# Attention scores: one operation per head for bias, maximum and sink in place of wide operations over four heads

## The reference, cut to what matters

```python
def windowed_gqa(q, k, v, sink, bias):
    ...
    s = jnp.einsum('bnqhgd,bnjhd->bnhgqj', qb, kb) * (HEAD_DIM ** -0.5) + bias
    s = jnp.where(jnp.asarray(valid)[None, :, None, None], s, -1e30)
    sink6 = sink.astype(jnp.float32)[None, None, :, :, None, None]
    m = jnp.maximum(jnp.max(s, axis=-1, keepdims=True), sink6)
    pe = jnp.exp(s - m)
    den = jnp.sum(pe, axis=-1, keepdims=True) + jnp.exp(sink6 - m)
    o = jnp.einsum('bnhgqj,bnjhd->bnqhgd', pe / den, vb)
```

## Time and profile before

| what | us |
|---|---|
| median of three runs | 1793.28 (1780.39 to 1795.96) |
| the profiled execution, its own time | 1783.18 |
| its span in the trace | 1781.1 |
| PE busy over the span | 1677.9 |
| DVE busy over the span | 904.8 |
| ACT busy over the span | 590.2 |
| first score matmul of the attention to the last `att_tok` | 651.8 to 787.8 |

### The profile page before, as it was taken

How to read it: one execution, slowest core, us unless ns; L and a number is a source line. 1 busy time by engine, 2 the same in 40 slices (tenths; PEclk the granted TensorE clock), 3 DMA queues, 4 the chain that set the end, 5 groups by cost and what they waited for, 6 DMA issues and landing times. The chain is left out here.

```text
span 1781.1 us, 26275 instructions
## 1 busy us (share of the span) xinstructions
PE 1677.9 (94%) x10034; PEld 1384.5 (78%) x10035; DVE 904.8 (51%) x998; ACT 590.2 (33%) x1015; POOL 409.2 (23%) x285
## 2 busy tenths in 40 slices
PE   7999999999999989999899999997999999997997
PEld 6878888877877767778788887885777777785786
DVE  5202777202044127742799325223777879952674
ACT  5211222231111126652344334113534343442332
POOL 1011111111111101002210022000265655653330
PEclk9999999999999989999789999998999999999999
DMA  6211222233455322107866434224767778744452
GB/s 222 78 58 60 80 79 80 100 90 117 133 183 169 118 74 62 32 31 234 261 198 166 165 126 138 83 72 146 297 224 256 276 280 303 282 170 142 142 189 95
DMA packets 117275, 267.70 MB, mean 150 GB/s; under 512 B 13044, under 2 KB 60868, under 8 KB 117181
## 3 DMA queue, kind: packets, MB, share of 16 engines
q1 hardware_dynamic: 101212, 211.60, 36.5%
q0 software_dynamic: 8320, 30.43, 5.1%
q10 hardware_dynamic: 7648, 24.35, 3.8%
HBM read 194.27 MB, written 72.07 MB: 150 GB/s over the span
## 5 line engine op out<-in xcount | busy, mean ns | idle before, releaser
L2228 DVE TENSOR_TENSOR ex_wlo<-ex_raw,ex_whi 128x1024 fp32r<-128x1024 f32 x102 | 156.1, 1532 | 7.6 <-ACT ex_whi L2222 4.3
L2224 DVE CAST ex_whi<-ex_raw 128x1024 fp32r<-128x1024 f32 x96 | 110.3, 1149 | 43.4 <-DMA ex_raw<-experts 38.5
L2816 PE MATMUL rt_p<-ex_whi,ex_xh 128*128 x280 | 113.6, 406 | 14.0 <-DVE ex_wlo L2228 8.6
L271 PE MATMUL rest_p<-hi_h,whi_in 128*128 128x512 f32 (+1 forms) x480 | 121.1, 361 | 0.0
L271 PE MATMUL rest_p<-lo_h,whi_in 128*128 128x512 f32 (+1 forms) x480 | 119.7, 357 | 0.0
L271 PE MATMUL rest_p<-hi_h,wlo_in 128*128 128x512 f32 (+1 forms) x480 | 119.5, 357 | 0.0
L2818 PE MATMUL rt_p<-ex_whi,ex_xl 128*128 x280 | 110.1, 393 | 0.0
L2817 PE MATMUL rt_p<-ex_wlo,ex_xh 128*128 x280 | 109.8, 392 | 0.0
L271 PEld LDWEIGHTS rest_p<-hi_h,whi_in 128*128 128x128 f32 x480 | 79.6, 188 | 21.6 <-issue 7.6
L945 POOL TENSOR_TENSOR wlo_in<-wraw_in,whi_in 128x1024 fp32r<-128x1024 f32 x18 | 43.9, 2437 | 227.5 <-ACT whi_in L908 227.5
L914 ACT ACTIVATE rest_out<-rest_p 128x1024 f32<-128x1024 f32 x20 | 20.5, 1026 | 214.2 <-PE rest_p L271 210.6
(11 more groups left out here) (420 smaller groups left out, 3981.9 us busy)
## 6 DMA issues: line engine op xcount, KB each, us to landing
ex_raw<-experts SPq DMA_DIRECT2D x96, 512.0 KB, 6.2
wraw_in<-units SPq DMA_DIRECT2D x36, 512.0 KB, 4.3
y_slots<-ex_y ACTq DMA_DIRECT2D x35, 512.0 KB, 4.4
rest<-rest_out SPq DMA_DIRECT2D x20, 640.0 KB, 5.5
scan_e<-erow SPq DMA_DIRECT2D x32, 256.0 KB, 5.0
xtok<-conv_tok SPq DMA_DIRECT2D x10, 640.0 KB, 3.4
z_x<-x SPq DMA_DIRECT2D x10, 512.0 KB, 4.0
ao_gate<-rest SPq DMA_DIRECT2D x8, 640.0 KB, 5.7
```

The lines of the kernel that those rows point to most:

```text
L271: mm = pe.matmul(out[:, n, 0:size], w[:, kk, :], h[:, kk, c:c + size], start=(kk == 0 and w is whi and h is hi), stop=(kk == ktiles - 1 an ...
L2224: eng.tensor_copy(self.hi[:, e % 2, n, :], self.raw[e % 2][:, n, :]).then_inc(self.w_hi[n], 1)
L2228: eng.tensor_tensor(self.lo[:, e % 2, n, :], self.raw[e % 2][:, n, :], self.hi[:, e % 2, n, :].bitcast(F32), ALU.subtract).then_inc(self.w ...
L2816: pe.matmul(gu[s][:, :], xh[s][:, kk, :], hi, start=(kk == 0), stop=False)
```

## The change

The scores get their bias, their scaling and their part in the maximum and sink in one `tensor_tensor_reduce` per head, which reads score_p from PSUM and a bias table that is now 8 times the bias: it writes -(score + bias) to `scores`, and the minimum of that row and the negative sink to `att_stat`. The four operations of a unit count `scored` one by one. The wide L1447, the TENSOR_REDUCE L1454 and L1456 go. The exponential takes the sign back with scale = -1, and waits for its own head's operation in place of the whole unit's `ready`; the sink's exponential now waits for `ready`. `scale(u - 2)` stays where it was: behind the operations on the scores of unit u.

```diff
--- before.py
+++ after.py
@@ -790,7 +790,7 @@
         dve.tensor_copy(self.line[:, :], self.bp[0][0:N_HEADS, :]).then_inc(self.line_copied, 1)
         for h in range(N_HEADS):
             dve.wait_ge(self.flipped, h + 1)
-            dve.tensor_copy(bias[:, 0, h, :], self.bp[h % 2][:, 0:BAND]).then_inc(self.copied, 1)
+            dve.tensor_scalar(bias[:, 0, h, :], self.bp[h % 2][:, 0:BAND], HEAD ** 0.5, None, ALU.mult).then_inc(self.copied, 1)
         dve.wait_ge(self.copied, N_HEADS)
         dve.sem_inc(done, 1)
         for v in (1, 2):
@@ -1280,10 +1280,10 @@
         pv_bank = ctx.enter_context(nc.psum_tensor("pv_p", [P, 512], F32))
         pv = pv_bank[:, 0:4 * (HEAD + 1)].rearrange("p (i e) -> p i e", i=4)
         ap_ = ctx.enter_context(nc.psum_tensor("att_t", [P, 4, P], F32))
-        names = ("v_zero", "v_turned", "v_copied", "sink_neg", "score_done", "scored", "step",
+        names = ("v_zero", "v_turned", "v_copied", "sink_neg", "score_done", "scored",
                  "probs", "turned", "pt_ready", "pv_done", "att_done", "att_turned", "att_hi_s",
                  "att_lo_s", "ready", "pv_step", "ones_set", "sunk")
-        (v_zero, v_turned, v_copied, sink_neg, score_done, scored, step, probs,
+        (v_zero, v_turned, v_copied, sink_neg, score_done, scored, probs,
          turned, pt_ready, pv_done, att_done, att_turned, att_hi_s, att_lo_s, ready, pv_step, ones_set, sunk) = k.sems(
              ctx, *(f"att_{n}" for n in names))
         ident = k.const[:, C_ID:C_ID + P]
@@ -1327,7 +1327,7 @@
                     pe.wait_ge(qk_in[s], 32 * (n // 2))
                 if u:
 
-                    pe.wait_ge(scored, u)
+                    pe.wait_ge(scored, 4 * u)
                 for m in range(2):
                     for g in range(N_KV):
                         mm = pe.matmul(sp_[:, 2 * g + m, 0:BAND], qs[g * HEAD:(g + 1) * HEAD, s, 2 * h + m, :],
@@ -1396,10 +1396,9 @@
             act.preload_act_table(ACT.Exp)
 
             def exp(u, i):
-                if i == 0:
-                    act.wait_ge(ready, u + 1)
+                act.wait_ge(scored, 4 * u + i + 1)
                 x = sc[:, u % 3, i, :]
-                act.activation(x, x, ACT.Exp, bias=st[:, u % 3, 1, i:i + 1]).then_inc(probs, 1)
+                act.activation(x, x, ACT.Exp, scale=-1.0, bias=st[:, u % 3, 1, i:i + 1]).then_inc(probs, 1)
 
             def copy(u, i):
                 j = 4 * u + i
@@ -1425,6 +1424,7 @@
                 copy(u, 0)
                 exp(u, 3)
                 copy(u, 1)
+                act.wait_ge(ready, u + 1)
                 act.activation(st[:, u % 3, 3, :], st[:, u % 3, 2, :], ACT.Exp).then_inc(sunk, 1)
                 copy(u, 2)
                 if u % 2 == 0 and u > 3:
@@ -1444,18 +1444,13 @@
                 if u >= 3:
 
                     dve.wait_ge(turned, 4 * (u - 2))
-                dve.scalar_tensor_tensor(out=sc[:, b, :, :].rearrange("p (g m) n -> p g m n", g=N_KV),
-                                         in0=sp_[:, :, 0:BAND].rearrange("p (g m) n -> p g m n", g=N_KV), scalar=HEAD ** -0.5,
-                                         in1=k.bias[:, table(u // 2), :, :].rearrange("p (g h m) n -> p h g m n", g=N_KV, h=2)[:, h, :, :, :],
-                                         op0=ALU.mult, op1=ALU.add).then_inc(scored, 1)
+                for i in range(4):
+                    j = 4 * (i // 2) + 2 * h + i % 2
+                    dve.tensor_tensor_reduce(sc[:, b, i, :], sp_[:, i, 0:BAND], k.bias[:, table(u // 2), j, :], -(HEAD ** -0.5),
+                                             nsink[:, j:j + 1], ALU.add, ALU.min, st[:, b, 1, i:i + 1]).then_inc(scored, 1)
                 if u >= 2:
                     scale(u - 2)
-                dve.wait_ge(scored, u + 1)
-                dve.tensor_reduce(st[:, b, 0, :], sc[:, b, :, :], AX.X, ALU.max).then_inc(step, 1)
-                dve.wait_ge(step, 2 * u + 1)
-                dve.scalar_tensor_tensor(out=pair(st[:, b, 1, :]), in0=pair(st[:, b, 0, :]), scalar=-1.0,
-                                         in1=of_unit(nsink[:, :], h), op0=ALU.mult, op1=ALU.min).then_inc(step, 1)
-                dve.wait_ge(step, 2 * u + 2)
+                dve.wait_ge(scored, 4 * u + 4)
                 dve.tensor_tensor(pair(st[:, b, 2, :]), pair(st[:, b, 1, :]), of_unit(sink[:, :], h), ALU.add).then_inc(ready, 1)
 
             def scale(u):
```

## The result

The changed kernel took 1797.86 us, median of 20 runs (1791.41 to 1807.31), against 1791.41 us for 20 runs of the kernel before (1780.39 to 1796.91). The ratio is 1.0041, with a 95% interval of 1.0027 to 1.0055: slower by 0.41%, some 7.3 us. Its profiled execution has a span of 1792.8 us.

The account below looks back on a forecast made before the run. PE sets the pace, tied to DVE in a loop in the attention. Ten loops growing by 0.76 us and eight by 0.15 less give 12.5 us; set between 1795.7 and 1805.8, the forecast is 1800 us, range 1785 to 1820.

Parts of the forecast that it names:

- The loop: Attention, PE and DVE: score, DVE's operations on the scores, `scale`, `weigh`, next score; 6.32 us per unit without `out`.
- x: How much later `scale` starts after the change: 0.76 us, between 0.24 and 1.55.
- T: Time from DVE's first operation on a unit's scores to the start of `scale`: from 1.68 to 2.44 us.
- 0.15 us of slack: In 8 units with `out`, `weigh` waits for ScalarE's copy, so DVE may finish 0.15 us later at no cost.
- The step: Time each of DVE's four per-head operations adds ahead of `scale`: 0.61 us.
- the write-out: DVE writing out the minimum after each per-head operation: 0.07 us, between 0 and 0.19.
- the sum: Attention's total added time, 10 units growing by x and 8 by x - 0.15: 12.5 us.
- case A: The forecast: the attention's loop grows by some 0.4 to 1.05 us, 6 to 18 us in all; chance 0.55.
- B: DVE's write-out and per-partition operand are hidden, x about 0.24, 3.1 us more, nearly no change; chance 0.2.
- C: Nothing overlaps between DVE's per-head operations, x 1.39 to 1.55, 23.8 to 26.7 us, slower by over 1%; chance 0.2.
- D: Faster: PE waited for the exponentials through ScalarE's copies, and they run earlier now; at most 3 us; chance 0.05.
- the forecast's base: Time of the kernel before, set between its profiled execution of 1783.18 us and a median 10.1 us above.

Follow-up runs that it names:

- experiments 3: The kernel before with its wide L1447 cut into four operations, one per head, maximum and sink still wide: 1790.49 us in one execution.
- experiment 4: The changed kernel with a constant (1e30) in place of the per-partition negative sink as start of the running minimum: 1788.10 us in one execution.
- experiment 7: The changed kernel with an unused maximum over 128 x 768 of the bias table added ahead of `scale`: 1827.98 us in one execution.
- experiment 5: The changed kernel with the exponentials' waits of the kernel before, the first of a unit waiting for `ready`: 1798.40 us in one execution.
- experiment 8: The changed kernel with score cut into two halves of two heads, one ahead of `weigh(u, 0)`: 1783.36 us, median of 12, ratio to before 0.9962.

## Why the prediction was right

*The place.* The loop was read rightly from the earlier trace rows, and it carried the change: wherever the clock was full, the period without `out` came out as 6.32 + x, within 0.02 us, in the four kernels below whose T differs from that of before. Units with `out` had 0.15 us of slack, as taken: 6.49 + 0.33 = 6.82 against 6.81.

| kernel | T, us | period without `out` | with `out` |
|---|---|---|---|
| before | 1.68 | 6.32 | 6.49 |
| before, cut in four | 1.87 | 6.51 | 6.51 |
| changed, constant for the sink | 1.92 | 6.57 | 6.56 |
| changed | 2.16 | 6.81 | 6.81 |
| changed, with 768 columns added (full clock) | 3.02 | 7.68 | 7.66 |
| either, with `scale` first | none | 6.13 | 6.49 |

*The size.* The step was put at 0.48 + 0.06 + 0.07 = 0.61 us and measured 0.54. The first two terms hold: cut alone 0.47, operand 0.06. The third, 0.07 us for the write-out, is the one that was mis-sized: experiments 3 and 4 leave 0.01 us for it and the minimum together, and in the trace the write-out starts in the same instant as the next operation. That makes T 2.16 us for 2.44, the period 6.81 for some 7.1, x 0.48 for 0.76 and the sum 7.4 us for 12.5. The prediction had 0 as the lower end of that term and said what it would take off the sum, 5.0 us; case A's span of x, 0.4 to 1.05, holds the result. That 1800 lies so near to 1797.86 is in part luck: the forecast's base was 1800 - 12.5 = 1787.5 us, and the longer series of before has its median at 1791.41; the two errors, 3.9 us low and 5.1 high, partly cancel.

(The Trainium skill, "VectorE: DVE Perf Modes", section "Two Vector instructions with no wait between them", counts an operation that writes out its accumulator as two instructions. The trace agrees: 80 rows of 84 ns. But they add next to nothing to the step of 0.54 us.)

*The rivals.* B, with x near 0.24, had the write-out right and the operand wrong; experiment 4, without the operand, has that x. C did not come: the next operation starts 0.08 us before the one ahead ends (706.50 + 0.62 against 707.04). (The section "The DRAIN you can't avoid" of the Trainium skill's page "VectorE: DVE Perf Modes" has the rule that the prediction gives for C, but adds that a next operation which is not held starts earlier; the 0.08 us agree with that addition, for operations with an accumulator too.) C's price was also too low: at x = 1.34 experiment 7 measured 36.6 us and not 23. By that, C's x of 1.39 to 1.55 would have brought the time above the range. D fell: the exponentials do not wait, and experiment 5 shows their waits to be worth nothing.

*Smaller points.* PE's wait for `att_tok` was to be in nearly all 18 units and some 20 us: 18 and 15.2. DVE's busy time was to fall by 10 to 20 us and fell by 25.1; the step, shorter by 0.07 us, makes 80 x 0.07 = 5.6 us of that. The bias tables' eight operations take the 558 ns of the copies.

## What to carry to other kernels

Find the loop before counting work: an engine with idle time in every unit can still set the pace, if one of its operations stands between two of the busy engine's; then the order on its queue can be worth more than its load. Here fusing took 35 us of maximum off DVE and put 0.48 us into each of 18 turns of the loop (8 of them had 0.15 us of slack), and the kernel became slower because the fused work stood ahead of the step that PE waited for; the same operations behind that step cost nothing. Finer operations paid where they let the producer be cut too, in experiment 8.

## What the runs showed of the hardware that was not expected

The write-out of a running minimum (84 ns) starts together with the next operation and lengthens a step by 0.01 us at most (0.48 against 0.47 us). A per-partition operand costs 0.06 us on an operation of 384 columns (615 against 554 ns). And waits of 1.5 to 1.9 us in every unit went with a granted clock of 0.87 to 0.93, and waits of up to 2.7 us with 0.74 to 0.87, in a stage that had run at 1.00 with waits of 0.6 to 1.04 us: in both runs the added stall cost more than its length, 36.6 us for 23 and 76.9 for 37.
